# Half of the merge-gate tiles move from the decode stage to the prompt's mLSTM stage

## The reference

```
z = einsum('btd,de->bte', h, w_in)          # 1024 -> 7*512 + 8 + 2*1024 columns
mq, mk, mv, mo, mif, dq, dk, dv, gm, gd = split_columns(z)
hm, C, n, m = mlstm_branch(mq, mk, mv, mo, mif, ...)    # chunked recurrence, then sigmoid(mo) * rms_norm(h)
hd, k_rows, v_rows = diff_branch(dq, dk, dv, ..., past_k, past_v)
merged = (sigmoid(gm) * einsum('btw,wd->btd', hm, w_proj_m)
          + sigmoid(gd) * einsum('btw,wd->btd', hd, w_proj_d))
y = einsum('btd,de->bte', merged, w_out)
```

## The kernel before

| step | line |
|---|---|
| gate matmuls, their sigmoid and their store | 1541, 1335, 1273 |
| key transposes, copy, scores | 1572, 1366, 1581 |
| state transposes, copy, product with q | 1654, 1399, 1641 |
| state update: product, VectorE's addition, weighted keys | 1678, 1522, 1515 |
| mLSTM chunk: key and value transposes, scores | 1943, 1948, 1953 |
| numerator, state product, output transposes | 1978, 1986, 1961 |
| attention columns: high part, low part | 1849, 1929 |
| chunk loads | 1762, 1764 |
| split_hi, split_lo, projection matmuls | 138, 142, 157 |

## Time and profile before

### The profile page before, as it was taken

How to read it: one execution, slowest core, us unless ns; L and a number is a source line. 1 busy time by engine, 2 the same in 40 slices (tenths; PEclk the granted TensorE clock), 3 DMA queues, 4 the chain that set the end, 5 groups by cost and what they waited for, 6 DMA issues and landing times. The chain is left out here.

```text
span 2055.0 us, 27831 instructions
## 1 busy us (share of the span) xinstructions
PE 1847.0 (90%) x11754; PEld 1772.1 (86%) x11754; DVE 764.8 (37%) x1009; ACT 498.6 (24%) x820; POOL 141.2 (7%) x208
## 2 busy tenths in 40 slices
PE   5999899999899999445999659999999999999994
PEld 4999788888799999444999649999999999999993
DVE  3421244454300114165441273443353444244435
ACT  4211243443322131222111252121121111211202
POOL 2000000000000000152000061000000000000000
PEclk7999999999998999777999859999999999999997
DMA  7655424222254222552241231101111111111005
GB/s 252 220 187 168 143 70 128 87 86 94 67 172 131 69 77 90 159 141 64 83 158 41 75 112 58 63 21 63 41 42 42 62 42 42 42 42 62 21 1 186
DMA packets 158709, 190.39 MB, mean 93 GB/s; under 512 B 13201, under 2 KB 137185, under 8 KB 158546
## 3 DMA queue, kind: packets, MB, share of 16 engines
q1 hardware_dynamic: 133992, 165.93, 25.0%
q10 hardware_dynamic: 23840, 22.44, 3.4%
q0 software_dynamic: 752, 0.16, 0.1%
HBM read 146.67 MB, written 41.83 MB: 92 GB/s over the span
## 5 line engine op out<-in xcount | busy, mean ns | idle before, releaser
L157 PE MATMUL ps<-acts_hi,w_hi 128*128 128x352 f32 x1488 | 325.2, 327 | 25.9 <-DVE acts_lo L2075 13.0
L157 PE MATMUL ps<-acts_hi,w_lo 128*128 128x352 f32 x1488 | 322.5, 324 | 0.0
L157 PE MATMUL ps<-acts_lo,w_hi 128*128 128x352 f32 x1488 | 322.0, 325 | 0.0
L157 PEld LDWEIGHTS ps<-acts_hi,w_hi 128*128 128x128 f32 x1488 | 254.5, 190 | 28.3 <-DVE acts_lo L2075 13.4
L157 PEld LDWEIGHTS ps<-acts_hi,w_lo 128*128 128x128 f32 x1488 | 256.9, 189 | 0.0
L157 PEld LDWEIGHTS ps<-acts_lo,w_hi 128*128 128x128 f32 x1488 | 254.4, 189 | 0.0
L142 DVE TENSOR_TENSOR w_lo<-w_raw,w_hi 128x2048 fp32r<-128x2048 f32 x63 | 144.1, 2288 | 171.9 <-ACT w_hi L138 171.9
L2546 DVE TENSOR_TENSOR f_t<-f_t,ps 128x1056 f32<-128x1056 f32 x88 | 110.3, 1254 | 167.8 <-PE ps L157 167.8
L138 ACT ACTIVATE w_hi<-w_raw 128x2048 fp32r<-128x2048 f32 x63 | 120.6, 1914 | 154.3 <-PE ps L157 152.0
L1113 PE MATMUL ps<-acts_hi,w_hi 128*128 128x352 f32 x384 | 133.6, 348 | 9.4 <-PEq L314 5.1
L1541 PE MATMUL ps<-acts_hi,w_hi 128*128 128x352 f32 x384 | 133.3, 347 | 4.4 <-PEq L894 4.0
(11 more groups left out here) (376 smaller groups left out, 2508.8 us busy)
## 6 DMA issues: line engine op xcount, KB each, us to landing
w_raw<-in_w_in SPq DMA_DIRECT2D x22, 1024.0 KB, 5.5
w_raw<-in_w_up SPq DMA_DIRECT2D x22, 1024.0 KB, 5.1
w_ada_chunks<-in_w_ada ACTq DMA_DIRECT2D x16, 1024.0 KB, 7.7
w_raw<-in_w_down SPq DMA_DIRECT2D x11, 1024.0 KB, 4.9
z_scratch<-out_z SPq DMA_DIRECT2D x48, 176.0 KB, 1.8
z_scratch<-squashed SPq DMA_DIRECT2D x48, 176.0 KB, 1.8
w_ada_chunks<-in_w_ada SPq DMA_DIRECT2D x8, 1024.0 KB, 8.7
z_scratch<-stage SPq DMA_DIRECT2D x12, 528.0 KB, 3.0
```

The lines of the kernel that those rows point to most:

```text
L157: mm = pe.matmul(ps[:, bank + b, 0:TB], w[wi][:, k, j * P:(j + 1) * P], (a_hi, a_lo)[ai][:, k, b * TB:(b + 1) * TB], start=(n == 0), stop= ...
```

## The change

Of the 48 gate tiles the decode keeps tiles 0 to 23, and its table of places is shorter: two steps over keys share one place, four steps over values, states or updates share one. Tiles 24 to 47 are made in the mLSTM block: two before the first chunk is prepared, then one before a chunk's numerator, one after its state product and, from the third chunk on, one after the output transposes. All of them use one PSUM bank, so each waits until ScalarE has taken out the one before, by a plain copy; the output transposes now share the bank of the value transposes. In the mLSTM block nothing is split any more. The prompt's columns stay in fp32 in a tensor `branch`, the o-gates are multiplied in place, and two of the four attention heads' columns are loaded there only in the merge block. The merge block splits `branch` row by row ahead of its first projection tile, which waits for it row by row, and gives `gate_d` its sigmoid on ScalarE after each load.

The decode's table of places:

```diff
-    AT_TOK, AT_K, AT_ROWS, AT_PT, AT_PV = 5, 7, 16, 17, 18
-    AT_O = AT_PV + DEC_B
-    AT_M, AT_C = AT_O + 1, AT_O + 2
-    AT_N2, AT_CU = AT_C + DEC_B + 1, AT_C + DEC_B + 4
+    DEC_TILES = GATE_TILES // 2
+    AT_TOK, AT_ROWS, AT_PT = 3, 9, 10
+    AT_K = [4 + b // 2 for b in range(DEC_B)] + [8]
+    AT_PV = [11 + b // 4 for b in range(DEC_B)]
+    AT_O, AT_M = 13, 14
+    AT_C = [15 + b // 4 for b in range(DEC_B)] + [17]
+    AT_N2 = 18
+    AT_CU = [20 + b // 4 for b in range(DEC_B)]
```

Ahead of the mLSTM block, its places, tiles 0 to 23 being done:

```diff
+    M_TILE0 = DEC_TILES + 2
+    AT_NUM = [M_TILE0 + 2 * c + 1 + max(0, c - 2) for c in CH]
+    AT_TR = [n + 1 for n in AT_NUM]
+    AT_NEXT = [n + (c >= 2) for c, n in enumerate(AT_TR)]
```

In the mLSTM block, SP:

```diff
-                for c in range(LS):
-                    load(c)
-                for c in range(2, H):
-                    ndv.wait(sp, ("br", c - 2))
-                    sp.dma_start(br_d[:, c % 2], BRANCH[c]).then_inc(n_br[c % 2], 16)
-                    npe.wait(sp, ("num", c + 1 - LS))
-                    load(c + 1)
...
+                def gates(t):
+                    gate_out(sp, t - 1, gate_raw[:, (t - 1) % 2, :])
+                    gate_weights(sp, t)
+
+                until = counted(gates, DEC_TILES + 1)
+                load(0)
+                load(1)
+                for h in range(H):
+                    sp.dma_start(mo_g[:, h], ZT[Z_MO + h, :, 0:SEQ]).then_inc(n_mo, 16)
+                load(2)
+                until(M_TILE0 + 1)
+                for h in range(2):
+                    sp.dma_start(br_d[:, h], BRANCH[h]).then_inc(n_br[h], 16)
+                for c in CH:
+                    until(AT_NUM[c])
+                    if c + LS < NCH:
+                        npe.wait(sp, ("num", c))
+                        load(c + LS)
+                    until(AT_NEXT[c])
```

In the mLSTM block, ScalarE:

```diff
+                def gates(t):
+                    act.wait_ge(tile_done, TILEG + t)
+                    act.wait_ge(gate_stored[(t - 1) % 2], 16 * ((t - 1) // 2))
+                    act.activation(gate_raw[:, (t - 1) % 2, :], ps[:, BG, 0:TB], ACT.Copy).then_inc(gate_evac, 1)
```

In the mLSTM block, TensorE:

```diff
+                def gates(t):
+                    pe.wait_ge(gate_evac, t)
+                    gate_tile(pe, t, BG)
+
+                until = counted(gates, DEC_TILES)
+                until(M_TILE0)
                 prepare(0)
                 for c in CH:
                     s = c % 2
                     if c + 1 < NCH:
                         prepare(c + 1)
+                    until(AT_NUM[c])
...
                     npe.done(mm, ("cu", c))
+                    until(AT_TR[c])
                     if c:
                         out_tr(c - 1)
+                    until(AT_NEXT[c])
```

In the merge block, ScalarE:

```diff
-                split_hi(act, 1, loads_of(PROJ0 + 1), TILE4)
                 for k in range(KT):
+                    if k == H:
+                        split_hi(act, 1, loads_of(PROJ0 + 1), TILE4)
+                    if k >= H + 2:
+                        act.wait_ge(n_br[k % 2], 32)
+                    act.activation(acts_hi[:, k, 0:SEQ], branch[:, k], ACT.Copy).then_inc(samples_hi, 1)
+                for k in range(KT):
+                    act.wait_ge(gate_loaded[1], 16 * (k + 1))
+                    act.activation(gate[1][:], gate[1][:], ACT.Sigmoid).then_inc(gate_open, 1)
```

In the merge block, VectorE:

```diff
-                split_lo(dve, 1, PROJ0 + 2)
+                for k in range(KT):
+                    if k == H:
+                        split_lo(dve, 1, PROJ0 + 2)
+                    dve.wait_ge(samples_hi, k + 2)
+                    dve.tensor_tensor(acts_lo[:, k, 0:SEQ], branch[:, k], acts_hi[:, k, 0:SEQ].bitcast(F32), ALU.subtract)\
+                        .then_inc(samples_lo, 1)
```

In the merge block, TensorE:

```diff
-                pe.wait_ge(samples_lo, 1)
...
-                                  acts_lo[:, 4 * g:4 * g + 4, :], 3 * g)
+                                  acts_lo[:, 4 * g:4 * g + 4, :], 3 * g, samples_lo if k == 0 else None, 2 + 4 * g)
```

More of the change, by code:

```diff
@@ L1205, in build, with counted, until, behind @@
     NK = NEWC + TS
+    def counted(part, first=0):
+        at_ = [first]
+        def until(n):
+            for t in range(at_[0], n):
+                part(t)
+            at_[0] = max(at_[0], n)
+        return until
+    def behind(t):
+        return GATE0 + (t - 1) // PER_CHUNK + 1 if (t - 1) % PER_CHUNK == 0 else None
+    def gate_tile(pe, t, bank):
+        c, j, b = t // PER_CHUNK, t // NTB % 2, t % NTB
+        if t % PER_CHUNK == 0:
+            pe.wait_ge(w_lo_ready, GATE0 + c + 1)
+        w = [x[:, c % 2, :].rearrange("p (k n) -> p k n", k=KT) for x in (w_hi, w_lo)]
+        order = products(KT)
+        for n, (k, wi, ai) in enumerate(order):
+            mm = pe.matmul(ps[:, bank, 0:TB], w[wi][:, k, j * P:(j + 1) * P],
+                           (acts_hi, acts_lo)[ai][:, k, b * TB:(b + 1) * TB],
+                           start=(n == 0), stop=(n == len(order) - 1))
+        mm.then_inc(tile_done, 1)
+    def gate_out(sp, t, src):
+        c, j, b = t // PER_CHUNK, t // NTB % 2, t % NTB
+        sp.wait_ge(gate_evac, t + 1)
+        sp.dma_start(ZT[Z_GM + 2 * c + j, :, b * TB:(b + 1) * TB], src).then_inc(gate_stored[t % 2], 16)
+    def gate_weights(sp, t):
+        n = behind(t)
+        if n is not None and n + 2 < PROJ0 + 2:
+            if n + 2 < PROJ0:
+                load_chunk(sp, n % 2, w_cols(I["w_in"][0], GATE_COL + (n + 2 - GATE0) * NC_), KT, n + 1)
+            else:
+                src = (I["w_proj_m"][0], I["w_proj_d"][0])[n % 2].rearrange("(k p) n -> p k n", p=P)
+                load_chunk(sp, n % 2, src[:, :, 0:CW // 4], W_MIX // P, n + 1)
     with ExitStack() as scope:
@@ L1268, in gates @@
                 def gates(t):
[L1270 to L1283, removed]
+                    gate_out(sp, t - 1, squashed[:, (t - 1) % 2, :])
+                    gate_weights(sp, t)
+                until = counted(gates, 1)
                 sp.dma_start(table[:], I["page_table"].rearrange("b g -> (b g)").unsqueeze(0)).then_inc(d_tables, 16)
@@ L1412, in gates @@
                 def gates(t):
-                    if t >= 1 and behind(t) is not None:
+                    if behind(t) is not None:
                         split_lo(dve, behind(t) % 2, behind(t) + 1)
-                until = counted(gates)
+                until = counted(gates, 1)
                 dvs.done(dve.memset(mv_tok[:, :, DH:PV1], 1.0), "one")
@@ L1679, in _ @@
                     pes.done(mm, ("cu", b))
-                until(GATE_TILES)
+                until(DEC_TILES)
     CH = range(NCH)
+    OPEN = [x for h in range(H) for x in (("mo", h), ("mog", h))]
     NPE_STEPS = ([("kT", 0), ("vT", 0), ("s", 0)]
@@ L2038, in gate_load @@
                     sp.dma_start(gate[1][:], ZT[Z_GD + k]).then_inc(gate_loaded[1], 16)
+                for h in range(2, H):
+                    sp.dma_start(branch[:, H + h], BRANCH[h]).then_inc(n_br[h % 2], 16)
                 gate_load(0)
```

196 lines of the change are left out of this document (93 added, 103 removed).

## The result

| | before | changed | predicted |
|---|---|---|---|
| median, same chip | 2058.78 us (4 runs) | 2079.53 us (4 runs, 2077.77 to 2080.89) | 2043 |
| ratio, 95% interval | | 1.0099 (1.0081 to 1.0116) | 0.9925 |
| span of the profiled execution | 2055.0 | 2076.0 | |
| decode block on TensorE | 276.3 | 247.4 (555.8 to 803.2) | 212.5 |
| end of the decode to the last mLSTM transpose | 121.7 | 161.3 (803.2 to 964.5) | 161.7 |

The kernel became 1.0% slower where 0.8% faster was forecast. Two of the three stages came out nearly as the sum had them. The decode gave back 28.9 us and not 63.8, and those 34.9 us are nearly the whole of the 36.5 by which the forecast was off. Two executions further down, one of the split-first version (3091.2 us) and one of the version with 28 tiles (2046.6 us), showed a lower granted clock than their fellows, and the ratios leave them out (the medians do not).

A forecast was written before the change was run, and what follows sets the result against it. TensorE was taken as full in the decode (275.82 of 276.30 us), with about 65 us idle in the mLSTM stage. Decode -63.8, mLSTM +40, merge +7.4 sum to -16.4 from 2056.7: 2040, stated as 2043 us, range 2019 to 2061.

The forecast's parts named there:

- Decode, tiles removed: Decode: 24 gate tiles leave TensorE's time line, 102.7 us of busy time, so 100.2 us come off.
- Decode, waits: Decode: waits at keys, states and state updates that lay under a tile now show, together 20.7 us.
- The 0.45 for the mask addition: Decode: one wait of 0.45 us for the mask addition ahead of the first key, part of the 20.7.
- Pages: Decode: key pages stay hidden; the prediction is wrong if pages end the waits of the key steps.
- Decode, clock: Decode: ten remaining lone gate tiles cost 6.0 us each through the slower clock, +15.7 us, bounds 0 and 26.
- The mLSTM stage: Tiles moved there make TensorE end at 994.7 where it ended at 954.6, +40 us; 17.4 us a chunk.
- above 0.9: mLSTM stage: sign that TensorE's granted clock would be above 0.9; below 0.85 the prediction is wrong.
- The wait before tile 27: mLSTM stage: sign of a TensorE wait ahead of tile 27 that a gate store ends.
- the one before tile 29: mLSTM stage: sign of a TensorE wait ahead of tile 29 that a gate store ends; start about 881.
- The merge: Merge: store wait +1, first projection tile +1.8, sigmoid ahead of weight splits +1.6 at row 3, +3 at row 7: +7.4 us.
- Rival 4: Slower: clock falls in the mLSTM chunks' gaps, ten decode tiles at 7.0 us: 2074, above 2064; chance 0.13.
- The rule weighed: Skill rule: gaps between matmul bursts bring 1.2 GHz, transposes don't count as busy; by it every lone tile starts slow.

The follow-up runs named there:

- split-first version: Changed kernel with the first half of the weight split put ahead of the sigmoid at merge rows 3 and 7: 2069.1 us, ratio 1.0069.
- version with 28 tiles: Changed kernel with 28 gate tiles in the decode as halves, 20 in the mLSTM stage, weight split ahead of the sigmoid: 2016.8 us, ratio 0.9804.

## Why the prediction was wrong

- *Decode, tiles removed, -100.2.* The tiles left as counted. Together with the next but one term, the slow clock on the lone tiles (+15.7), it says -84.5; from start to start the decode's gate tiles went from 201.5 to 117.2 us, -84.3.
- *Decode, waits, +20.7.* Right: 18.3 measured, and 2.4 are the ends of ten groups of transposes, 0.24 us each, that no longer lie under a tile. The 0.45 for the mask addition did not appear. Pages ended none of them; ScalarE's copies (1.11 us a key, 0.69 a state) and the weighted keys (1.37 an update) did.
- **The step that failed: *Decode, clock*, +15.7 with bounds 0 and 26.** It counted the slow clock on the ten lone gate tiles alone. Those I had right: nine of them took 5.0 to 6.8 us, 6.0 in the mean, as I took it (the tenth runs into the tiles behind it). But the clock fell during the small products *ahead* of them, and these run at it too. I treated their 4.2 us a key and 1.2 us a state as fixed. That is +33.0 us by the six groups above: scores +10.7, value products +9.2, updates +4.9, state products +3.4, transposes +3.0 and +1.8. Busy times leave out that a matmul's end lies under the next one's start. Counted from start to start, the six groups went from 65.2 to 101.7 us: +36.5, of which 2.4 are the ends of the transposes above and 34 stood in the sum at nothing. Then the account closes: -84.3 for the tiles, +36.5 for the groups and +18.5 for the waits make -29.3, where -28.9 was measured. My upper bound was no bound: it priced all ten lone tiles at the slow clock and none of the 608 small matmuls.
- *The mLSTM stage, +40.* +39.6 measured, chunk to chunk 17.4 to 18.5 us for 17.4, clock 0.94 for "above 0.9". The wait before tile 27 was there (3.62 us), ended by the evacuation; the one before tile 29 wasn't, and the first two chunks' loads were waited for, 3.3 and 4.1 us. Tile 29 started 51.3 us after the decode's end where the sum had 48, and the rest took 110.0 us where it had 113.7. That the two errors cancel is luck; the mechanism, a stage filled up to TensorE's own work at the full clock, held.
- *The merge, +7.4.* The first tile 2.6 later for 2.8, row 3 +1.95 for 1.6, row 7 +4.4 for 3, of which 1.35 is the slower clock behind row 3's wait, which the sum left out.
- *Rivals.* Rival 4 named the clock and a time of 2074, near the measured one, but in the wrong place: it had the clock fall in the chunks' gaps, where it stayed up, and the ten decode tiles at 7.0, where they stayed at 6.0.
- *The rule weighed.* By "TensorE: Matmul & The Clock Gate" of the Trainium skill, Part 1, gaps between bursts bring the engine to 1.2 GHz. The trace agrees where there are gaps (the first three matmuls took 1.25 us behind the 4 us waits and 0.74 behind those of 0.9 us). But the value window had no gap and stood at 0.58: a reader who only looks for idle time would, like me, not look there.

## What to carry to other kernels

When large matmuls are taken from between small ones, price the small ones at the lower clock as well: the trace of before shows them only at the clock that the large ones kept up. Leave a piece of dense work at every place where there was one, and cut the pieces smaller before you thin out the places. An activation that waits for a load belongs behind a split whose input has already landed.

## What the runs showed that I had not expected

- A fully busy TensorE can stay at 1.2 GHz: 36.50 of 36.50 us busy in the value window at a granted clock of 0.58, and 17.00 of 17.00 at 0.50 in its first half, when most of it was products of four columns.
- Such a product costs nearly twice as much there though it has only four columns: 1.84 us for 16 at the full clock, 3.41 at the other. The time of its weight load goes the same way, 192 ns in the median before and 333 after.
- Coming back was harder than staying, in the one execution that shows it: eight large matmuls behind each value step did not raise the clock in three steps (0.53 in that stretch), and the same eight held it for three steps (1.00) once it had risen during a whole tile of 24.
